# Where the modulation chunks stand among the units of attention

## What is computed

```python
silu_c, silu_cc = jax.nn.silu(c), jax.nn.silu(c_ctx)
for l in range(DEPTH):
    mod_lat = (silu_c @ ada_w[l] + ada_b[l])[:, None, :]
    mod_ctx = silu_cc @ ada_w[l] + ada_b[l]
    ...
# layer 0, per head pair and block of 128 queries:
s = jnp.einsum('bqhmd,bthmd->bhmqt', dq, dk) * ATTN_SCALE
p = jax.nn.softmax(s.astype(jnp.float32), axis=-1)
a = (p[:, :, 0] - lam * p[:, :, 1]).astype(dv.dtype)
d_out = jnp.einsum('bhqt,bthe->bqhe', a, dv)
d_out = rms_norm(d_out, subln_g) * (1.0 - lam_init)
```

## Time and profile before

| | us |
|---|---|
| Median of three runs | 1246.57 |
| Lowest and highest | 1245.77 and 1247.6 |
| Span of the profiled execution, first to last instruction | 1244.3 |
| Median less this span (no time of its own is given for the profiled execution) | 2.3 |
| TensorE busy | 1174.4 (94%) |
| VectorE busy | 617.3 (50%) |
| ScalarE busy | 564.2 (45%) |

### The profile page before, as it was taken

The page is one execution under the profiler, slowest core; times in us unless marked ns, Lnnn a source line. Parts: engine busy times, 40 slices in busy tenths (PEclk is TensorE's granted clock), DMA queues, the critical chain, the costliest instruction groups (busy, mean ns, idle before and its releaser), DMA issues.

```text
span 1244.3 us, 17650 instructions
## 1 busy us (share of the span) xinstructions
PE 1174.4 (94%) x6999; PEld 914.8 (74%) x6999; DVE 617.3 (50%) x973; ACT 564.2 (45%) x1061; POOL 122.5 (10%) x117
## 2 busy tenths in 40 slices
PE   5899989989889999999999899999979998999997
PEld 3577744558468888888888648788869966888886
DVE  2532258662452333232222276489976535666553
ACT  2622247763462233223222274866344535665642
POOL 0030320110000111111000000010015100111100
PEclk9899989999999999999999989999979999999999
DMA  9654656652463333333333462234103032766662
GB/s 343 213 165 144 180 184 222 209 131 85 136 169 89 97 102 99 88 101 93 93 93 97 149 156 72 66 85 119 51 4 82 22 90 80 197 181 187 189 195 68
DMA packets 222748, 159.51 MB, mean 128 GB/s; under 512 B 14778, under 2 KB 191308, under 8 KB 222668
## 3 DMA queue, kind: packets, MB, share of 16 engines
q1 hardware_dynamic: 221888, 158.11, 43.0%
q10 hardware_dynamic: 780, 0.29, 0.1%
HBM read 157.33 MB, written 1.05 MB: 127 GB/s over the span
## 4 chain that ended last, share of the span: by engine, by line
PE 80%; DVE 8%; ACT 7%; issue 2%; DMA 1%; SPq 1%; POOL 0%; DVEq 0%; ACTq 0%; POOLq 0%
PE bank L1407 43%; PE bank L1418 6%; PE bank L1588 5%; PE bank L1419 3%; PE bank L1394 2%; PE bank L1515 2%; PE bank L1658 2%; ACT h_work L1783 2%; PE bank L1496 1%; PE bank L1668 1%; DVE blocks L1045 1%; DVE outer L1043 1%; PE bank L803 1%; PE bank L1465 1%; DMA w_raw<-in_ada_w 1%
## 5 line engine op out<-in xcount | busy, mean ns | idle before, releaser
L1407 PE MATMUL bank<-h_both,w_hi 128*128 128x512 f32 x1296 | 403.7, 393 | 2.5 <-issue 2.5
L1997 DVE TENSOR_TENSOR w_lo<-w_raw,w_hi 128x1024 fp32r<-128x1024 f32 (+1 forms) x161 | 200.8, 1249 | 229.7 <-ACT w_hi L1750 228.7
L1407 PEld LDWEIGHTS bank<-h_both,w_hi 128*128 128x128 f32 x1296 | 242.1, 188 | 53.4 <-issue 3.5
L1407 PE MATMUL bank<-h_both,w_lo 128*128 128x512 f32 x648 | 252.5, 390 | 0.0
L1750 ACT ACTIVATE w_hi<-w_raw 128x1024 fp32r<-128x1024 f32 (+1 forms) x161 | 167.0, 1040 | 76.9 <-PE bank L1407 52.9
L1407 PEld LDWEIGHTS bank<-h_both,w_lo 128*128 128x128 f32 x648 | 121.6, 188 | 25.8
L1419 PE MATMUL bank<-h_both,w_lo 128*128 128x256 f32 x308 | 86.5, 281 | 0.0
L1418 PE MATMUL bank<-h_both,w_hi 128*128 128x512 f32 x231 | 83.0, 398 | 1.4 <-DVE h_both L2050 1.0
L1407 PE MATMUL bank<-act_hi,w_hi 128*128 128x512 f32 x176 | 68.5, 389 | 0.0
L1407 PE MATMUL bank<-act_lo,w_hi 128*128 128x512 f32 x176 | 68.5, 389 | 0.0
L1407 PE MATMUL bank<-act_hi,w_lo 128*128 128x512 f32 x176 | 68.5, 389 | 0.0
(11 more groups left out here) (301 smaller groups left out, 1844.3 us busy)
## 6 DMA issues: line engine op xcount, KB each, us to landing
w_raw<-in_ada_w SPq DMA_DIRECT2D x96, 512.0 KB, 5.0
w_raw<-in_ffn_w_gate_up SPq DMA_DIRECT2D x88, 512.0 KB, 3.8
w_raw<-in_ffn_w_down SPq DMA_DIRECT2D x38, 512.0 KB, 3.7
w_raw<-in_gdn_w_in SPq DMA_DIRECT2D x32, 512.0 KB, 4.0
w_raw<-in_attn_w_in SPq DMA_DIRECT2D x14, 512.0 KB, 3.9
w_raw<-in_gdn_w_out SPq DMA_DIRECT2D x8, 512.0 KB, 5.3
w_raw<-in_ffn_w_down SPq DMA_DIRECT2D x8, 384.0 KB, 3.3
w_raw<-in_attn_w_in SPq DMA_DIRECT2D x8, 256.0 KB, 3.5
```

What stands on the lines that cost most here:

```text
L1407: m = nc.tensor.matmul(dst, stationary(a, k), moving(b, k), start=(first and k == kk[0] and a == b == 0), stop=(last and k == kk[-1] and a ...
L1997: nc.vector.tensor_tensor(w_lo[where[key] % N_RAW][:, 0:tiles, 0:w], raw_slot(key)[:, 0:tiles, 0:w], w_hi[hi_slot(m)][:, 0:tiles, 0:w].bit ...
```

## The change

The same 40 chunks are taken in attention in the same order, but four behind the scores of every third unit (4, 7, ... 28), with a pair at unit 1 and a pair at unit 30. Chunks 36 and 37 move from unit 2 to unit 4, 40 and 41 from unit 5 to unit 7, and so on with each second pair of two, up to 68 and 69, which move from unit 26 to unit 28; 72 and 73 move from unit 29 to unit 30. The other pairs stay where they are. So units 4, 7, ... 28 hold two pairs each, and units 2, 5, 8, ... 29 none. With it, the turning of batch 1 moves from unit 11 to unit 13 and that of batch 2 from unit 29 to unit 30; the two copies to `ada_rows` stay in units 10 and 28. The order of the weight stream is unchanged.

```diff
-ADA_UNITS = [n for n in range(1, len(ATT_UNITS)) if n % 3][:20]
+ADA_UNITS = {1: (34, 2), 30: (72, 2)}
+ADA_UNITS.update({1 + 3 * n: (32 + 4 * n, 4) for n in range(1, 10)})
 GAP_COUNTS = (2, 3, 6)
-ADA_GAPS = {"gap0": 34 + 2 * len(ADA_UNITS), "gap1": 34 + 2 * len(ADA_UNITS) + sum(GAP_COUNTS)}
+ADA_GAPS = {"gap0": 74, "gap1": 74 + sum(GAP_COUNTS)}
...
     if phase == "att" and step in ADA_UNITS:
-        return pair(34, ADA_UNITS.index(step))
+        first, count = ADA_UNITS[step]
+        return list(range(first, first + count))
```

## The result

The changed kernel takes 1252.79 us (median of five runs, 1250.87 to 1253.76), the kernel before 1246.57 (five runs too, 1245.77 to 1247.6). The ratio is 1.0046, 95% interval 1.0036 to 1.0057: slower by about 5.7 us. I had forecast 1248.8, slower by 2.2, and a range up to 1251.5. The sign was that of the sum, the size was not.

The account below looks back on a forecast made before the run. TensorE, busy 94% of the span, bounds the kernel, with a loop through three engines pacing attention's first half. Units 1 to 20 (+1.3) and 20 to 31 (+0.9) add 2.2 us to 1246.57: 1248.8, range 1244.5 to 1251.5.

Parts of the forecast that it names:

- Price of a pair and of a merge: TensorE in attention: a pair behind scores costs 0.98 us, each further pair of a run 0.86; nine merges save 1.1.
- The first two St: First half of attention: the first St about 0.2 us late, the second within 0.1 us of before.
- The chain of ScalarE at 20: Unit 20's pair lay under ScalarE's chain and now stands uncovered in iteration 22: +0.98 us, less 0.1 for jitter.
- S(20): Scores of unit 20, closing units 1 to 20: estimated 1.3 us late, bounds -0.7 and +4.5.
- Unit 24: Second half of attention: without the pair of 23, TensorE waits 0.5 us on ScalarE's chain, so +0.35 us.
- The end: From the scores of unit 31 to the output projection: 14.03 us behind ScalarE, moves rigidly, zero.
- The copies to `ada_rows`: Units 10 and 28: VectorE waits for two pairs, covered by lag, so zero; otherwise 0.86 us at unit 10.
- Transfers: Weight chunks keep about 9 us of notice; output weights are issued later but before their use: zero.
- Iteration 13: Turning and two pairs, 2.83 us against 0.98; next scores 1.7 late, VectorE's backlog covering most, about 0.3 arriving at the maxima.
- the second half: Units 20 to 31: lost covers at 20 and 24 less three merges, +0.9 us, bounds -0.36 and +1.6.
- My sign of starving: Rival in attention: two-pair runs starve VectorE, 1252.0 us, chance 0.13; VectorE's waits for scores past 14 us would show error.
- The fall of the clock: Rival: longer TensorE waits at 12 and 20 bring back the 1.2 GHz clock, +3 us, 1251.8, chance 0.05.

Follow-up runs that it names:

- the kernel with added scores: The changed kernel with the scores of unit 12 computed three times over in place of once, four extra matmuls: 1250.49 us, ratio 1.0029.

## Why the prediction was wrong

**What held.** *Price of a pair and of a merge:* 0.98 and 0.86, runs of 1.84 us. *The first two St:* counted from S(1), each 0.4 us late, where I had 0.2 and 0.1. *The chain of ScalarE at 20:* 3.06 us behind S(20) with or without a pair, and the pair was worth 0.84. *Unit 24:* a wait of 0.55 against 0.5. *The end:* 14.03 us, rigid. *The copies to `ada_rows`:* VectorE waited once, 0.4 us. *Transfers:* no wait of TensorE for a chunk.

**What failed first: a mis-sized term.** Iteration 13: "VectorE has a backlog that covers most of that, and about 0.3 us arrives". At a clock of 1.00, in the kernel with added scores, S(13) to S(14) grew by 1.84 us (4.49 against 2.65), near my 2.83 - 0.98 = 1.85. But 0.9 us more than at the second St arrived at the third: 1.3 us late, where I had 0.5. The turning alone is worth 0.85 to 0.9 there (two runs). The backlog can be read from the maxima (L2190). TensorE and VectorE at units 14 and 15 in the kernel before:

```profile
209.64 1.13 PE L1658 MATMUL bank<-k_sb,q_sb 64*128 64x512 f32 x4
211.83 1.28 DVE L2190 TENSOR_REDUCE stats<-bank 128x1 f32<-128x512 f32 x2
...
213.16 1.13 PE L1658 MATMUL bank<-k_sb,q_sb 64*128 64x512 f32 x4
214.32 1.29 DVE L2190 TENSOR_REDUCE stats<-bank 128x1 f32<-128x512 f32 x2
```

and at unit 15 in the kernel with added scores:

```profile
215.28 1.13 PE L1664 MATMUL bank<-k_sb,q_sb 64*128 64x512 f32 x4
...
216.44 1.29 DVE L2196 TENSOR_REDUCE stats<-bank 128x1 f32<-128x512 f32 x2
```

Before, the maxima of 14 start 2.19 us behind their scores and those of 15 only 1.16. Where VectorE waits for the scores of 14, as with added scores (212.74 to 213.90, wait 0.22) and in the changed kernel (3.08), the distance is 1.16 too. So VectorE's lag was 1.03 us at unit 14 and nothing at 15, one unit on. There TensorE's delay arrives whole: 0.39 from in front of iteration 13, 0.99 for the turning, 0.86 for the merged pair, less 0.98 for the pair that has left 14, is 1.26; S(15) was 1.25 us late and the third St 1.27. In place of my 0.3, the turning's 0.99 less the merge's 0.12 has to stand in the sum. (With the turning VectorE's own bias adds come to 13 as well, 0.90 us with added scores, 211.53 to 212.43. They don't set the pace: VectorE still waits 0.22 us for scores behind them, and 0.51 us for S(15) in the kernel with the pair of unit 2 left out.) I had inferred the backlog from waits for scores that were never over 2.4 us; a longest wait doesn't say how large the lag is at the unit in question.

S(20) is then 2.1 us late in place of 1.3, and the second half adds 1.1 in place of 0.9: 3.2 in place of 2.2. This alone would have given 1249.8, inside my range. My sign of starving, waits for scores past 14 us, did come (15.7), but with the clock at 1.00 they are 12.8 (the kernel with added scores).

**What failed second: a rival priced right and ranked last.** The fall of the clock stood among the rivals at +3 us with a chance of 0.05, with the waits at 12 named as its place; it is 3.2 us and came in both profiles of the changed kernel. It is what takes the time out of the range; the sum had it at nothing. I weighed it down by the end of attention, where TensorE idled 4.9 of 15 us at 1.00. That row was real, and the same waits (1.18 and 1.70 us) show a clock of 1.00 in the changed kernel up to 284 us. It spoke for one place only. I had also worked out the wait at V(8) too lightly: with neither chunk nor turning in 11 and 12 it is 1.66 us, where before it was 0.54, and it deserved its own term. With both, 2.2 + 1.0 + 3.2 = 6.4 us in the profile; by the ratios over all executions it is about 5.1 to 5.7, which would fit a clock that holds in some.

**What stays open.** Why a wait of 1.66 us at 203.7 lets the clock fall and 1.70 us near 278 does not. In the changed kernel TensorE was busy for 0.66 of 2 us in front of the fall; that is all the rows say. In front of the projection one and the same wait, 2.53 us, was followed by a low clock in nine profiles of twelve and not in the other three, so the length of a wait isn't all of it. Nor is it known in which share of executions the clock falls at 207.

## What to carry to other kernels

Filler work is not free or costly by its amount but by what stands around it: put it under the longest chain of the other engines (here St's, and the end of attention), never in front of the instruction that such a chain waits for. When an edit leaves an iteration with less work, work out the wait that opens there as a term of its own, and price a low clock behind it. And follow what hangs on a chunk's number: the turning moved with chunk 48 into iteration 13 in several of these kernels, and where it could be taken alone it cost 0.85 to 0.9 us, nearly as much as a pair.

## What I had not expected of the hardware

Matmuls added in front of a wait made attention 3.2 us shorter (medians 1250.49 against 1252.7), because the clock stayed at 2.4 GHz: 6.8 us at 1.2 GHz cost 3.2 us. What goes with the fall in the profiles is the size of the wait in front of V(8): a wait of 1.66 or 1.67 us was followed by the fall in four profiles of four, a wait of 0.54 to 0.80 us at the same place or none at all in none of ten, the three of the kernel before among them.
